# Where one query tile is loaded, and how five others are dealt out, in a two-block kernel with a gathered expert layer

## The chip, the cores and the metric

The kernel runs on one core of one Trainium2 chip. Its engines are TensorE (PE, with PEld for its weight loads), VectorE (DVE), ScalarE (ACT), GpSimd (POOL) and SyncE (SP, which only issues transfers here); 16 DMA engines move the data. The metric is the device time of one execution in microseconds (us). Before the change it is 1383.3 us, the median of three runs (1383.12 to 1384.93).

## What is computed

Two transformer blocks, one after the other, on 256 tokens of width 1024, all in float32. The part that this change touches is the second half of the first block, a product-key expert layer ("PEER"). Cut to what matters, the reference is:

```python
q = h @ wq                                   # h: normed x, 256 x 1024; wq: 1024 x 2048 (8 heads x 2 x 128)
s1, s2 = q[.., 0] @ keys[h, 0].T, q[.., 1] @ keys[h, 1].T      # 128 scores on each side
v1, i1 = top_k(s1, 16); v2, i2 = top_k(s2, 16)
top_s, pos = top_k(v1[:, None] + v2[None, :], 16)              # 16 best pairs of 256
idx = i1 * 128 + i2;  g = softmax(top_s)                        # 8 heads x 16 = 128 experts a token
a = <u[idx], h>;  x = x + sum(gelu(a) * g * v[idx])             # u, v: 16384 x 1024 each
x = x + sigmoid(norm(x) @ ple_gate) * (p @ ple_proj)            # "PLE", right behind it
```

Each token needs 128 rows of `u` and of `v`. They lie side by side in one table, so an expert's row has 2048 floats (8 KB).

## The kernel before, in words

The 256 tokens are two blocks of 128 (b = 0, 1), one token on each of 128 partitions. Each block needs 128 gathers. Gather k fetches, for every token of the block, the table row of one of its experts: 128 rows of 8 KB, 1.05 MB. The 256 gathers are issued one by one by POOL (line L1421) into a ring of ten places in SBUF (`pair_ring`; gather k goes to place (k + 1) mod 10, so k = 7 and 8 go to places 8 and 9, and k = 9 to place 0). Gather k of 10 or more waits until TensorE is done with gather k - 10 (`pair_free`).

Four gathers are a batch (64 batches, m = 0 to 63; block 0 has batches 0 to 31). For each batch VectorE takes four dot products with `u` (L1824), forms the weights with one tanh of ScalarE between (L1229), ScalarE builds four diagonal matrices (L1235), and TensorE multiplies each with `v` and adds to two PSUM banks (L804: two matmuls of 128x512 a gather, eight a batch).

Which rows to fetch comes from the routing: queries (TensorE), scores against the keys (TensorE, L759), and top-k searches (VectorE, L1726 to L1791). The 2048 query columns are four tiles, `peer_q0` to `peer_q3`, each for a pair of heads, 1024x512 floats (2 MB). The routing of a block is thus four parts (b, q). In block 0, parts (0,0), (0,1) and (0,2) are multiplied ahead of the first batch, whole. The other five are dealt out: after each batch TensorE does a quarter of a query product (`dealt`, L748, eight matmuls of 128x128), and after four quarters the scores. VectorE's search pieces are dealt out in the same way (`route_list`). All engines run their instructions in the order written; nothing is rescheduled.

Weight tiles come through a ring of three places (`wring`, 2 MB each), loaded by SP in the order of `tile_list` (L451). A tile is issued once the tile three before it in that list has had its last use. In the list the tiles here are `out0`, `out1` (the projection ahead of the expert layer), `peer_q0` to `peer_q3`, `ple_proj` (1 MB), `ple0`, `ple1`, and then tiles of the second block. So `peer_q2` can be issued only when `out1` has had its last product, and `peer_q3` when `peer_q0` has had the one for block 1.

Of the kernel before, what the change touches and what calls it, by code (L numbers as in the profile page):

```python
# [20 lines left out]
P = 128  # L21
S = 256
NB = S // P
D = 1024
KD = D // P
# [19 lines left out]
ADA_PARTS = (0, 1, 2, 3, 6, 7, 8, 9, 4, 5, 10, 11)  # L45
ADA_COLS = 8
FF_ADA = {1: 10, 2: 11}
PLE_PROJ, PLE_TURN, PLE_GATE, PLE_NORM, PLE_LAST = 36, 35, 40, 51, 54
GELU_C = 0.7978845608028654


# [25 lines left out]
def route_list():  # L77

    after = {}
    starts = {(0, 1): 0, (0, 2): 6, (0, 3): 14, (1, 0): 20, (1, 1): 26, (1, 2): 34, (1, 3): 42}  # L80
    for (b, q), m in starts.items():
        for piece, step in enumerate((0, 1, 2, 3, 4) if m == 0 else (0, 1, 3, 4, 5)):
            after.setdefault(m + step, []).append((b, q, piece))
    return after
# [2 lines left out]
ROUTE_AFTER = route_list()  # L87
BEST_AFTER = {m: p[:2] for m, pieces in ROUTE_AFTER.items() for p in pieces if p[2] == 3}

QUERY_FROM = {1: (1, 0), 5: (1, 1), 9: (0, 3), 14: (1, 2), 19: (1, 3)}  # L90

SEARCH = [(b, q) for b in range(NB) for q in range(PAIRS)]
SC_SLOT = {(0, 0): 0, (0, 1): 1, (0, 2): 2, (1, 0): 3, (0, 3): 0, (1, 1): 1, (1, 2): 2, (1, 3): 0}
# [3 lines left out]
def tile_list():  # L97


    ada = [(f"ada{i}", KD, 512, "w_ada", 0, 512 * ADA_PARTS[i]) for i in range(12)]  # L100
    at, t_in = 0, {}
    for n, w in (("q", 512), ("kv", 256), ("hq", 512), ("hf", 512), ("hb", 512), ("hi", 512), ("hg", 512),
                 ("g0", 512), ("g1", 512), ("g2", 512), ("g3", 512)):
        t_in[n] = ("in_" + n, KD, w, "w_in", 0, at)
        at += w
    t = [t_in[n] for n in ("hf", "hb", "q", "kv", "hq", "hi", "hg")]
    t += [ada[0], ada[1], t_in["g0"], ada[2], t_in["g1"], ada[3], t_in["g2"], ada[4], t_in["g3"], ada[5]]
    t += [("up_att", 4, D, "w_up_att", 0, 0)] + ada[6:ADA_COLS]
    t += [(f"out{i}", KD, 512, "w_out", 0, 512 * i) for i in range(2)]
    t += [(f"peer_q{i}", KD, 512, "peer_wq", 0, 512 * i) for i in range(4)]  # L110
    t += [("ple_proj", 2, D, "ple_proj", 0, 0)]
    t += [(f"ple{i}", KD, 512, "ple_gate", 0, 512 * i) for i in range(2)]
    t += [("in2_" + n, KD, 512, "w_in_2", 0, 512 * i) for i, n in enumerate(("q", "k", "v", "qm", "km"))]
    t += [("in2_if", KD, 64, "w_if", 0, 0), ("in2_vm", KD, 512, "w_in_2", 0, 512 * 5), ada[8]]
    t += [("in2_og", KD, 512, "w_in_2", 0, 512 * 6)] + ada[9:10]
    t += [(f"out2_{i}", KD, 512, "w_out_2", 0, 512 * i) for i in range(2)]
    for i in range(6):
        w = min(512, FF - 512 * i)
        t += [(f"gate{i}", KD, w, "w_gate", 0, 512 * i), (f"up{i}", KD, w, "w_up", 0, 512 * i)]
        if i in FF_ADA:  # L120
            t += [ada[FF_ADA[i]]]
    t += [(f"down{i}", min(4, FC - 4 * i), D, "w_down", 512 * i, 0) for i in range(6)]
    return t
# [6 lines left out]
def product_list():  # L130
# [4 lines left out]
    def half(n, b):  # L135
        return [(n, b, h) for h in range(2)]
# [23 lines left out]
    p += [("out0", 0), ("ada_col",), ("out1", 0)]  # L160
    p += half("n2T", 0) + [("out0", 1), ("peer_q0", 0, 0), ("keys", 0, 0, 0), ("peer_q0", 0, 1), ("keys", 0, 0, 1), ("out1", 1)]
    p += [("peer_q1", 0), ("peer_q2", 0), ("keys", 0, 1), ("keys", 0, 2)] + half("n2T", 1)
    for b, q in QUERY_FROM.values():
        p += [(f"peer_q{q}", b), ("keys", b, q)]
    p += half("experts", 0)
    p += half("n3T", 0) + [("ple_proj", b, h) for b in range(NB) for h in range(2)] + [("ple0", 0), ("ple1", 0)]
    p += half("n4T", 0) + half("experts", 1)
    p += half("n3T", 1) + [("ple0", 1), ("ple1", 1), ("in2_q", 0), ("in2_k", 0)] + half("n4T", 1)
# [46 lines left out]
def two_blocks(nc, a, out):  # L215

    with ExitStack() as ctx:
# [67 lines left out]
            return (k + 1) % RING  # L285

        sc = {pair: at(big, 20480 + 512 * n, 512).rearrange("p (n k) -> p n k", n=4) for pair, n in SC_SLOT.items()}
        subkeys = at(big, 22528, 2 * PH * NKEYS)
        h2T = [at(big, lo, D).rearrange("p (c t) -> p c t", c=KD) for lo in (26048, 27072)]
        pqT = at(big, 28096, 512).rearrange("p (n t) -> p n t", n=4)  # L290
# [72 lines left out]
        down_used, ada_used = sem("down_used"), sem("ada_used")  # L363
        x_landed = [sem(f"x_landed{b}") for b in range(NB)]
        ident_landed, const_landed, lane_landed = sem("ident_landed"), sem("const_landed"), sem("lane_landed")
        keys_landed = sem("keys_landed")
        rows_landed, mask_landed, pT_landed = sem("rows_landed"), sem("mask_landed"), sem("pT_landed")
        gain_landed, row_landed, row_added = sem("gain_landed"), sem("row_landed"), sem("row_added")
        ms_ready, rstd_ready, h_ready = sem("ms_ready"), sem("rstd_ready"), sem("h_ready")
# [57 lines left out]
        def _(sp):  # L427
# [3 lines left out]
            for n, (name, k, w, src, r0, c0) in enumerate(TILES):  # L431
# [12 lines left out]
                    sp.dma_start(up_hg, a["w_up_hg"].rearrange("(c p) n -> p c n", p=P)).then_inc(up_hg_landed, 16)  # L444
                if name == "in2_q":
                    sp.wait_ge(pair_free, (BATCHES - 1) * BATCH - 2)
                if name == "out0":
                    wait_product(sp, "g_A", 0, 1)
                    sp.dma_start(subkeys, a["subkeys"]).then_inc(keys_landed, 16)
                slot = n % W_SLOTS * TILE  # L450
                sp.dma_start(wring[:, slot:slot + k * w].rearrange("p (c n) -> p c n", c=k),  # L451
                             a[src][r0:r0 + k * P, :].rearrange("(c p) n -> p c n", p=P)[:, :, c0:c0 + w])\
                  .then_inc(tile_landed[n % W_SLOTS], 16)
                if n == 0:
                    sp.dma_start(x[:, 1, :], a["x"][P:S, :]).then_inc(x_landed[1], 16)
                if n == 1:
# [13 lines left out]
        def _(pe):  # L470
# [268 lines left out]
                pe.wait_ge(h_ready, 3 + b)  # L739
                turn("n2T", h_t, [b])  # L740

            def query(name, b, parts=range(4)):

                wt = tile(name, KD, 512)
                o = begin(name, b) if parts[0] == 0 else ps[:, BANK[(name, b)], :]
                for n in parts:
                    for c in range(KD):
                        last = nc.tensor.matmul(o[:, n * P:(n + 1) * P], wt[:, c, n * P:(n + 1) * P], h2T[b][:, c, :],  # L748
                                                start=(c == 0), stop=(c == KD - 1))
                if parts[-1] == 3:  # L750
                    last.then_inc(product_done, 1)

            def score(b, q):
# [66 lines left out]

            def dealt(m):
                for m0, (b, q) in QUERY_FROM.items():
                    if 0 <= m - m0 < 4:
                        query(f"peer_q{q}", b, range(m - m0, m - m0 + 1))
                    elif m - m0 == 4:
                        score(b, q)

            for m in range(1, HALF_BATCHES):
# [25 lines left out]

            for m in range(HALF_BATCHES, BATCHES):
                experts(m, banks)
                if m == PLE_TURN:
                    pe.wait_ge(h_ready, 5)
                    turn("n3T", h_t, [0])
                    pe.wait_ge(pT_landed, 16)  # L860
# [212 lines left out]
        def _(act):  # L1073
# [179 lines left out]
            def query_dealt(m):  # L1253

                for m0, (b, q) in QUERY_FROM.items():
                    if m - 1 == m0 + 3:
                        query_out(b, q)
                    if m - 1 == m0 + 4:
                        scores_out(b, q)

            exp_and_tanh()
# [22 lines left out]
            for m in range(HALF_BATCHES, BATCHES):  # L1284
# [3 lines left out]
                if m == HALF_BATCHES + 1:  # L1288
                    log_and_exp()
                    rms(2, 0)  # L1290
                    exp_and_tanh()
                if 0 <= m - 1 - PLE_PROJ < 4:
                    b, h = (m - 1 - PLE_PROJ) // 2, (m - 1 - PLE_PROJ) % 2
                    move(pp[:, b, h * 512:(h + 1) * 512], "ple_proj", b, h)
# [94 lines left out]
        def _(pool):  # L1389
# [22 lines left out]
            for k in range(NB * SLOTS):  # L1412
                if k == SLOTS // PAIRS // 2:
                    pool.wait_ge(indexed, 2)
                elif k % (SLOTS // PAIRS) == 0:
                    pool.wait_ge(indexed, k // (SLOTS // PAIRS) + (2 if k else 1))
                if ring_at(k) == 0 and k < RING:
                    wait_product(pool, "out1", 1)
                if k >= RING:
# [733 lines left out]
```

## Time and profile before

| | |
|---|---|
| median of three runs | 1383.3 us |
| the profiled execution's own time | 1384.18 us |
| its span (first to last instruction) | 1382.4 us |
| PE busy | 1241.1 us (90%) |
| DVE busy | 741.8 us (54%) |
| ACT busy | 231.6 us (17%) |
| POOL busy | 324.2 us (23%) |
| software-issued DMA queue (the gathers) | 270.29 MB |
| hardware-issued DMA queue (all weight tiles) | 127.88 MB |

The profile is of one execution on the chip. The granted clock is TensorE's, as a share of full speed. A wait for several semaphores is put down to the one that came last. The gathers run from 277 us to about 955 us of the span, so this stage is half of the kernel. A busy share averaged over the whole span says little about one stage; the rows below are therefore mostly of that stage.

### The profile page before, as it was taken

What the parts mean: (1) busy time and instruction counts of PE and PEld (TensorE: products, weight loads), DVE (VectorE), ACT (ScalarE), POOL (GpSimd) and SP (SyncE); (2) the same over time, 40 slices, a digit from 0 to 9 for tenths busy, and PEclk for the clock granted to TensorE, in tenths of its full rate; (3) what the DMA queues carried; (4) which work ended last, traced back from release to release, by engine and by line L of the source; (5) the groups of instructions that cost most, each with busy time, mean ns of one, the idle gap of its engine ahead of it and who ended that gap; (6) DMA issues with size and microseconds to landing.
All of it is one profiled execution on the core that took longest, in us unless ns stands there. A gap on an engine that the chain in (4) does not pass through costs nothing.

```text
span 1382.4 us, 12732 instructions
## 1 busy us (share of the span) xinstructions
PE 1241.1 (90%) x4624; PEld 742.5 (54%) x4624; DVE 741.8 (54%) x1777; ACT 231.6 (17%) x596; POOL 324.2 (23%) x273
## 2 busy tenths in 40 slices
PE   6999999978889888778798887787999899999998
PEld 6766887554444444323343333333466558888743
DVE  2766633369676777777786865653244632230001
ACT  2132210111211111112221112111201421000000
POOL 0100000034444445354445445451000000000000
PEclk9999999999999999999899999889999899999999
DMA  8445587299999999999999999996435324564531
GB/s 293 154 153 183 183 304 290 69 385 397 382 420 421 421 416 421 416 421 418 421 412 422 408 413 421 419 420 257 137 129 191 138 112 163 181 244 132 195 144 39
DMA packets 98670, 398.99 MB, mean 289 GB/s; under 512 B 6384, under 2 KB 9840, under 8 KB 65712
## 3 DMA queue, kind: packets, MB, share of 16 engines
q0 software_dynamic: 37376, 270.29, 47.5%
q1 hardware_dynamic: 61232, 127.88, 25.9%
q8 instruction: 38, 0.62, 0.2%
q14 instruction: 24, 0.20, 0.0%
HBM read 397.10 MB, written 1.05 MB: 288 GB/s over the span
## 4 chain that ended last, share of the span: by engine, by line
PE 59%; DMA 23%; DVE 13%; ACT 2%; issue 2%; POOL 1%; SPq 0%; DVEq 0%; ACTq 0%
DMA big<-in_peer_uv,idx_t 21%; PE ps L521 17%; PE ps L509 10%; PE ps L804 10%; DVE big L1824 6%; PE ps L1064 5%; PE ps L619 3%; PE ps L694 2%; PE ps L1024 2%; PE ps L537 1%; PE ps L748 1%; DMA wring<-in_peer_wq 1%; PE ps L600 1%; PE ps L725 1%; POOL big L1421 1%
## 5 line engine op out<-in xcount | busy, mean ns | idle before, releaser
L804 PE MATMUL ps<-big,rows 128*128 128x512 f32 x1024 | 487.1, 632 | 110.6 <-ACT rows L1235 110.6
L804 PEld LDWEIGHTS ps<-big,rows 128*128 128x128 f32 x1024 | 201.7, 202 | 378.3 <-issue 378.1
L1421 POOL DMA_INDIRECT big<-in_peer_uv,idx_t x256 | 311.1, 1215 | 382.6 <-PE ps L804 331.5
L1824 DVE CUSTOM_DVE_ANT_0 big<-big 128x1024 f32<-128x1024 f32 x256 | 307.9, 1224 | 146.2 <-DMA big<-in_peer_uv,idx_t 142.8
L521 PE MATMUL ps<-big,wring 128*128 128x256 f32 x1088 | 237.4, 379 | 0.0
L521 PEld LDWEIGHTS ps<-big,wring 128*128 128x128 f32 x1088 | 205.9, 190 | 31.4 <-issue 3.9
L509 PE MATMUL ps<-wring,big 128*128 128x512 f32 (+1 forms) x336 | 142.4, 581 | 4.4 <-DVE big L1950 4.4
L509 PEld LDWEIGHTS ps<-wring,big 128*128 128x128 f32 x336 | 64.1, 193 | 75.9 <-issue 74.5
L1229 ACT ACTIVATE small<-small 128x4 f32<-128x4 f32 x64 | 13.2, 206 | 507.5 <-DVE small L1829 507.5
L1235 ACT ACTIVATE rows<-const,small 128x128 f32<-128x128 f32 x256 | 81.8, 390 | 19.6 <-DVE small L1833 18.4
L1064 PE MATMUL ps<-wring,big 128*128 128x512 f32 x176 | 75.7, 592 | 0.0
L1432 POOL TENSOR_TENSOR big<-big,rows 128x1024 f32<-128x1024 f32 x2 | 5.1, 2539 | 291.4 <-ACT big L1109 291.4
L748 PEld LDWEIGHTS ps<-big,wring 128*128 128x128 f32 x448 | 55.1, 198 | 17.0 <-issue 9.1
L748 PE MATMUL ps<-big,wring 128*128 128x128 f32 x448 | 55.5, 281 | 7.8 <-DMA wring<-in_peer_wq 7.8
L1109 ACT ACTIVATE big<-ps 128x512 f32<-128x512 f32 (+1 forms) x65 | 35.1, 579 | 124.6 <-PE ps L509 27.0
L1064 PEld LDWEIGHTS ps<-wring,big 128*128 128x128 f32 x176 | 33.4, 190 | 41.7 <-issue 41.6
L2016 DVE SCALAR_TENSOR_TENSOR big<-ps,big 128x512 f32<-128x512 f32 x8 | 5.5, 692 | 92.7 <-PE ps L1064 70.6
L2059 DVE TENSOR_TENSOR big<-big,ps 128x512 f32<-128x512 f32 x11 | 7.6, 688 | 82.1 <-PE ps L521 74.8
L619 PE MATMUL ps<-big,wring 128*128 128x128 f32 x384 | 45.4, 281 | 4.0 <-DMA wring<-in_w_in 3.0
L619 PEld LDWEIGHTS ps<-big,wring 128*128 128x128 f32 x384 | 44.9, 198 | 5.1 <-issue 3.9
L1401 POOL DMA_DIRECT2D rows<-in_norm_ffn x1 | 0.7, 686 | 138.8 <-DVE big L1677 138.8
L1024 PE MATMUL ps<-wring,big 128*128 128x512 f32 x64 | 28.0, 592 | 0.0
(251 smaller groups left out, 923.0 us busy)
## 6 DMA issues: line engine op xcount, KB each, us to landing
wring<-in_w_in SPq DMA_DIRECT2D x17, 2048.0 KB, 8.4
wring<-in_w_ada SPq DMA_DIRECT2D x12, 2048.0 KB, 8.3
wring<-in_w_gate SPq DMA_DIRECT2D x5, 2048.0 KB, 7.8
wring<-in_w_up SPq DMA_DIRECT2D x5, 2048.0 KB, 7.7
wring<-in_w_down SPq DMA_DIRECT2D x5, 2048.0 KB, 7.8
wring<-in_w_out SPq DMA_DIRECT2D x4, 2048.0 KB, 8.8
wring<-in_peer_wq SPq DMA_DIRECT2D x4, 2048.0 KB, 10.1
big<-in_peer_uv,idx_t POOLq DMA_INDIRECT x256, 13.4
```

The costliest lines, as they stand in the source:

```text
L509: last = nc.tensor.matmul(o[:, 0:w], lhs[:, c, b * P:(b + 1) * P], wt[:, c, c0:c0 + w], start=(c == 0), stop=(c == k - 1))
L521: last = nc.tensor.matmul(o[:, c2 * S:(c2 + 1) * S], wt[:, c, n0:n0 + P], src[:, c, :], start=(c == 0), stop=(c == KD - 1))
L619: last = nc.tensor.matmul(o[:, c2 * S + b * P:c2 * S + (b + 1) * P], wt[:, c, n0:n0 + P], src[:, c, b * P:(b + 1) * P], start=(c == 0), st ...
L694: last = nc.tensor.matmul(o[:, c2 * S:(c2 + 1) * S], wt[:, c, n0:n0 + P], lhs[:, c, :], start=(c == 0), stop=(c == 3))
L748: last = nc.tensor.matmul(o[:, n * P:(n + 1) * P], wt[:, c, n * P:(n + 1) * P], h2T[b][:, c, :], start=(c == 0), stop=(c == KD - 1))
L804: last = nc.tensor.matmul(banks[h], diag[:, k % DIAGS, :], v_part[:, ring_at(k), h * 512:(h + 1) * 512], start=False, stop=(k % SLOTS == S ...
L1024: last = nc.tensor.matmul(o, hT2[:, c, b * P:(b + 1) * P], wt[:, c, :], start=(c == 0), stop=(c == KD - 1))
L1064: last = nc.tensor.matmul(o, gT[:, f, b * P:(b + 1) * P], wt[:, c, h * 512:(h + 1) * 512], start=(f == 0), stop=(f == FC - 1))
L1109: nc.scalar.activation(dst, bank(name, n) if src is None else src, ACT.Copy).then_inc(emptied(*name), 1)
L1235: nc.scalar.activation(diag[:, k % DIAGS, :], ident, ACT.Copy, scale=w_now[:, at_w:at_w + 1])\
L1421: pool.indirect_dma_start(pair_ring[:, ring_at(k), :], None, a["peer_uv"], bass.IndirectOffsetOnAxis(idx_t[:, k:k + 1], 0))\
L1824: nc.vector.tensor_tensor_reduce(u_part[:, ring_at(k), :], u_part[:, ring_at(k), :], h_t[:, b, :], 1.0, 0.0, ALU.mult, ALU.add, a_dot[:, i ...
```

## The change

It has four edits, all in the expert stage.

1. The tile `peer_q2` for block 0 gets its own load, issued behind `peer_q0`, once the small product `ada_col` is done. It goes to the place of ring rows 8 and 9 (`q2_home`), which the gathers k = 7 and 8 use first. These two gathers (and k = 9 behind them in POOL's order) wait until the block-0 product with `peer_q2` is done.
2. In the list of ring tiles, `peer_q3` now comes ahead of `peer_q2`. `peer_q3` waits for the last use of `out1` and also for the landing of gather k = 9. `peer_q2` is loaded a second time, for block 1, behind it. One tile more is loaded in all.
3. The five dealt queries are in the order (0,3), (1,0), (1,1), (1,2), (1,3) instead of (1,0), (1,1), (0,3), (1,2), (1,3), each in eighths (four matmuls) over eight batches, from batches 1, 9, 17, 25 and 33, instead of in quarters from batches 1, 5, 9, 14 and 19. The search pieces of (1,1), (1,2) and (1,3) start two batches later.
4. The PLE steps move from batches 35 to 54 to batches 41 to 59, with the same distances but for one: the projection now starts in the batch of the transpose instead of the one behind it.

The core of the diff:

```diff
-PLE_PROJ, PLE_TURN, PLE_GATE, PLE_NORM, PLE_LAST = 36, 35, 40, 51, 54
+PLE_PROJ, PLE_TURN, PLE_GATE, PLE_NORM, PLE_LAST = 41, 41, 45, 56, 59
-    starts = {(0, 1): 0, (0, 2): 6, (0, 3): 14, (1, 0): 20, (1, 1): 26, (1, 2): 34, (1, 3): 42}
+    starts = {(0, 1): 0, (0, 2): 6, (0, 3): 14, (1, 0): 20, (1, 1): 28, (1, 2): 36, (1, 3): 44}
-QUERY_FROM = {1: (1, 0), 5: (1, 1), 9: (0, 3), 14: (1, 2), 19: (1, 3)}
+QUERY_FROM = {1: (0, 3), 9: (1, 0), 17: (1, 1), 25: (1, 2), 33: (1, 3)}
+PIECES = 8
-    t += [(f"peer_q{i}", KD, 512, "peer_wq", 0, 512 * i) for i in range(4)]
+    t += [(f"peer_q{i}", KD, 512, "peer_wq", 0, 512 * i) for i in (0, 1, 3, 2)]
+        q2_home = at(big, 8 * 2 * D, TILE).rearrange("p (c n) -> p c n", c=KD)
...
+                if name == "peer_q3":
+                    sp.wait_ge(pair_landed[ring_at(RING - 1)], 16)
...
+                if name == "peer_q0":
+                    wait_product(sp, "ada_col")
+                    sp.dma_start(q2_home, a["peer_wq"].rearrange("(c p) n -> p c n", p=P)[:, :, 2 * 512:3 * 512])\
+                      .then_inc(q2_landed, 16)
...
-            def query(name, b, parts=range(4)):
-                wt = tile(name, KD, 512)
-                o = begin(name, b) if parts[0] == 0 else ps[:, BANK[(name, b)], :]
-                for n in parts:
-                    for c in range(KD):
+            def query(name, b, pieces=range(PIECES)):
+                if (name, b) == ("peer_q2", 0):
+                    pe.wait_ge(q2_landed, 16)
+                    wt = q2_home
+                else:
+                    wt = tile(name, KD, 512)
+                o = reserved(name, b) if pieces[0] == 0 else ps[:, BANK[(name, b)], :]
+                for piece in pieces:
+                    n, c0 = piece // 2, piece % 2 * 4
+                    for c in range(c0, c0 + 4):
...
+                if ring_at(k) in (8, 9) and k < RING:
+                    wait_product(pool, "peer_q2", 0)
```

On SyncE, the issues from the last `w_out` tile to the two `ple_gate` tiles. Before (`wring` is the weight ring, `in_peer_wq` the query weights):

```order
L451 DMA wring<-in_w_out 128x8x512 [waits ada_used]
L451 DMA wring<-in_peer_wq 128x8x512 [waits product_done] x4
L451 DMA wring<-in_ple_proj 128x2x1024 [waits product_done]
L451 DMA wring<-in_ple_gate 128x8x512 [waits product_done] x2
L451 DMA wring<-in_w_in 128x8x512 [waits pair_free,product_done]
```

After (`pair_landed0` is raised by gather k = 9):

```order
L456 DMA wring<-in_w_out 128x8x512 [waits ada_used]
L456 DMA wring<-in_peer_wq 128x8x512 [waits product_done]
L461 DMA big<-in_peer_wq 128x8x512 [waits product_done]
L456 DMA wring<-in_peer_wq 128x8x512 [waits product_done]
L456 DMA wring<-in_peer_wq 128x8x512 [waits pair_landed0,product_done]
L456 DMA wring<-in_peer_wq 128x8x512 [waits product_done]
L456 DMA wring<-in_ple_proj 128x2x1024 [waits product_done]
```

Five issues of query weights stand where four stood; the fourth of them, `peer_q3`, is tied to a gather's landing.

On TensorE, batch 1 (the last of its gathers), the dealt piece behind it, and the first gather of batch 2. Before:

```order
L804 MATMUL ps<-big,rows 128x512 [waits diag_built,pair_landed8]
L804 MATMUL ps<-big,rows 128x512
L748 MATMUL ps<-big,wring 128x128 [waits bank_emptied1,tile_landed1]
L748 MATMUL ps<-big,wring 128x128 x7
L804 MATMUL ps<-big,rows 128x512 [waits diag_built,pair_landed9]
```

After:

```order
L819 MATMUL ps<-big,rows 128x512 [waits diag_built,pair_landed8]
L819 MATMUL ps<-big,rows 128x512
L762 MATMUL ps<-big,wring 128x128 [waits bank_emptied1,tile_landed0]
L762 MATMUL ps<-big,wring 128x128 x3
L819 MATMUL ps<-big,rows 128x512 [waits diag_built,pair_landed9]
```

The piece behind batch 1 has half the matmuls, and it reads place 0 of the weight ring, where `peer_q3` lands, instead of place 1, where `peer_q0` has lain since before the stage. All of batch 2 stands behind it.

On POOL, the first gathers. Before:

```order
L1421 DMA big<-in_peer_uv,idx_t 128x2048 [waits indexed]
L1421 DMA big<-in_peer_uv,idx_t 128x2048 x8
L1421 DMA big<-in_peer_uv,idx_t 128x2048 [waits product_done]
L1421 DMA big<-in_peer_uv,idx_t 128x2048 [waits pair_free] x6
L1421 DMA big<-in_peer_uv,idx_t 128x2048 [waits pair_free,indexed]
```

After:

```order
L1440 DMA big<-in_peer_uv,idx_t 128x2048 [waits indexed]
L1440 DMA big<-in_peer_uv,idx_t 128x2048 x6
L1440 DMA big<-in_peer_uv,idx_t 128x2048 [waits product_done] x3
L1440 DMA big<-in_peer_uv,idx_t 128x2048 [waits pair_free] x6
L1440 DMA big<-in_peer_uv,idx_t 128x2048 [waits pair_free,indexed]
```

Seven gathers instead of nine are free of a wait for a product; k = 7 and 8 now wait for that of `peer_q2`, k = 9 for that of `out1` as before.

## Rows read from the trace of the kernel before

**Rows 1.** The page: the chain of waits, by engine and by line.

```profile
PE 59%; DMA 23%; DVE 13%; ACT 2%; issue 2%; POOL 1%; SPq 0%; DVEq 0%; ACTq 0%
```

**Rows 2.** Windows: stretch; busy us of PE, PEld, DVE, ACT, POOL; clock; DMA share; GB/s.

```profile
276.00:308.00 32.00, 22.85 (x150) 19.47 (x149) 21.37 (x80) 6.19 (x14) 11.21 (x11) 0.89 0.96 387
308.00:332.00 24.00, 21.32 (x74) 11.30 (x73) 21.66 (x65) 4.42 (x13) 12.35 (x10) 1.00 0.98 371
332.00:348.00 16.00, 12.46 (x51) 7.39 (x50) 14.88 (x41) 3.09 (x11) 5.61 (x6) 0.96 1.01 421
348.00:364.00 16.00, 16.00 (x49) 8.02 (x48) 10.10 (x28) 2.95 (x10) 8.80 (x7) 0.94 0.90 344
690.00:712.00 22.00, 22.00 (x50) 9.42 (x49) 19.50 (x54) 4.16 (x13) 10.70 (x11) 0.97 1.00 405
790.00:800.00 10.00, 9.33 (x22) 4.00 (x21) 9.42 (x23) 1.48 (x5) 4.91 (x4) 0.98 0.95 347
800.00:944.00 144.00, 116.23 (x247) 48.77 (x246) 86.01 (x194) 25.58 (x77) 69.81 (x58) 0.92 1.01 421
```

**Rows 3.** Timeline of PE: start us, us, engine, line, operation, tiles, [idle before, releaser].

```profile
276.42 7.31 PE L748 MATMUL ps<-big,wring 128*128 128x128 f32 x64
291.49 9.28 PE L748 MATMUL ps<-big,wring 128*128 128x128 f32 x64 [7.76 <-DMA wring<-in_peer_wq]
300.61 1.06 PE L759 MATMUL ps<-big 128*128 128x128 f32 x8
304.77 7.10 PE L804 MATMUL ps<-big,rows 128*128 128x512 f32 x16 [1.39 <-ACT rows L1235]
315.31 7.11 PE L804 MATMUL ps<-big,rows 128*128 128x512 f32 x16 [1.67 <-ACT rows L1235]
322.25 1.95 PE L748 MATMUL ps<-big,wring 128*128 128x128 f32 x16
346.52 8.80 PE L804 MATMUL ps<-big,rows 128*128 128x512 f32 x16 [2.02 <-ACT rows L1235]
```

**Rows 4.** Timeline of DVE: last dot product and weights of batch 0; of a later batch.

```profile
295.01 1.23 DVE L1824 CUSTOM_DVE_ANT_0 big<-big 128x1024 f32<-128x1024 f32 x1 [1.25 <-DMA big<-in_peer_uv,idx_t]
304.02 0.16 DVE L1833 SCALAR_TENSOR_TENSOR small<-small 128x4 f32<-128x4 f32 x1 [7.11 <-ACT small L1229]
...
772.71 1.23 DVE L1824 CUSTOM_DVE_ANT_0 big<-big 128x1024 f32<-128x1024 f32 x1 [1.26 <-DMA big<-in_peer_uv,idx_t]
...
774.88 0.16 DVE L1833 SCALAR_TENSOR_TENSOR small<-small 128x4 f32<-128x4 f32 x1 [0.27 <-ACT small L1229]
```

**Rows 5.** Timeline of POOL: gathers k = 0, 10 and 26.

```profile
277.32 1.04 POOL L1421 DMA_INDIRECT big<-in_peer_uv,idx_t  x1 [27.89 <-DVE idx_t L1781]
306.99 0.94 POOL L1421 DMA_INDIRECT big<-in_peer_uv,idx_t  x1 [16.67 <-PE ps L804]
350.43 1.53 POOL L1421 DMA_INDIRECT big<-in_peer_uv,idx_t  x1 [5.94 <-PE ps L804]
```

**Rows 6.** DMA queues in 281 to 282 us: packets, MB, share.

```profile
q1 hardware_dynamic: 188, 0.39, 99.8%
q0 software_dynamic: 7, 0.06, 13.8%
```

**Rows 7.** DMA queues in 370 to 376 us.

```profile
q0 software_dynamic: 262, 1.88, 76.7%
q1 hardware_dynamic: 262, 0.54, 23.4%
```

**Rows 8.** The same view, 382 to 388 us: the end of that tile.

```profile
q1 hardware_dynamic: 115, 0.20, 9.0%
```

**Rows 9.** Half-microsecond windows around gather k = 26 (columns of rows 2).

```profile
351.50:352.00 0.50, 0.50 (x2) 0.19 (x1) 0.30 (x3) 0.20 (x1) 0.47 (x1) 1.00 0.19 82
352.50:353.00 0.50, 0.50 (x2) 0.19 (x1) 0.50 (x1) 0.50 (x3) 0.50 (x1) 1.00 1.32 229
```

**Rows 10.** The chain: start us, us, what (the load of `peer_q2`).

```profile
276.62 14.37 DMA wring<-in_peer_wq
```

**Rows 11.** SP's issue of `peer_q3` at 357.1 us: issue to landing.

```profile
L451 SPq DMA_DIRECT2D wring<-in_peer_wq x1: 367/367/367, 357.1 to 357.1; - x1
DMA to landing us min/median/max: 29.7/29.7/29.7
```

**Rows 12.** Timeline of DVE at 780 us: second half of a PLE addition.

```profile
780.43 0.69 DVE L1853 SCALAR_TENSOR_TENSOR x_t<-big,x_t 128x512 f32<-128x512 f32 x1
```

More of the change, by code:

```diff
@@ L162, in product_list @@
     p += [("peer_q1", 0), ("peer_q2", 0), ("keys", 0, 1), ("keys", 0, 2)] + half("n2T", 1)
-    for b, q in QUERY_FROM.values():
+    for m0, (b, q) in QUERY_FROM.items():
+        if m0 + PIECES - 1 == HALF_BATCHES:
+            p += half("experts", 0)
         p += [(f"peer_q{q}", b), ("keys", b, q)]
-    p += half("experts", 0)
     p += half("n3T", 0) + [("ple_proj", b, h) for b in range(NB) for h in range(2)] + [("ple0", 0), ("ple1", 0)]
@@ L365, in two_blocks @@
         ident_landed, const_landed, lane_landed = sem("ident_landed"), sem("const_landed"), sem("lane_landed")
-        keys_landed = sem("keys_landed")
+        keys_landed, q2_landed = sem("keys_landed"), sem("q2_landed")
         rows_landed, mask_landed, pT_landed = sem("rows_landed"), sem("mask_landed"), sem("pT_landed")
@@ L740, in turn_query @@
                 turn("n2T", h_t, [b])
-            def query(name, b, parts=range(4)):
-                wt = tile(name, KD, 512)
-                o = begin(name, b) if parts[0] == 0 else ps[:, BANK[(name, b)], :]
-                for n in parts:
-                    for c in range(KD):
+            def query(name, b, pieces=range(PIECES)):
[8 more added lines that the diff above has]
+                    for c in range(c0, c0 + 4):
                         last = nc.tensor.matmul(o[:, n * P:(n + 1) * P], wt[:, c, n * P:(n + 1) * P], h2T[b][:, c, :],
                                                 start=(c == 0), stop=(c == KD - 1))
-                if parts[-1] == 3:
+                if pieces[-1] == PIECES - 1:
+                    begin(name, b)
                     last.then_inc(product_done, 1)
@@ L822, in dealt @@
                 for m0, (b, q) in QUERY_FROM.items():
-                    if 0 <= m - m0 < 4:
+                    if 0 <= m - m0 < PIECES:
                         query(f"peer_q{q}", b, range(m - m0, m - m0 + 1))
-                    elif m - m0 == 4:
+                    elif m - m0 == PIECES:
                         score(b, q)
@@ L856, in _ @@
                 experts(m, banks)
+                dealt(m)
                 if m == PLE_TURN:
@@ L1255, in query_dealt @@
                 for m0, (b, q) in QUERY_FROM.items():
-                    if m - 1 == m0 + 3:
+                    if m - 1 == m0 + PIECES - 1:
                         query_out(b, q)
-                    if m - 1 == m0 + 4:
+                    if m - 1 == m0 + PIECES:
                         scores_out(b, q)
@@ L1291, in _ @@
                     exp_and_tanh()
+                query_dealt(m)
                 if 0 <= m - 1 - PLE_PROJ < 4:
```

## The prediction, as it was put on record

> **What bounds the kernel now.** I read the chain of waits first. It gives TensorE 59%, DMA 23% and VectorE 13% [rows 1], which is an average over stages. So the next view is the table of windows over the expert stage [rows 2]. The reader is to see that the DMA share is 1.01 wherever the rate is 421 GB/s (332 to 348 us, 800 to 944 us), while PE and DVE have idle time there. The stage is bound by the bytes that it moves, and its length is bytes divided by 421 GB/s plus the time in which DMA is short of work. An edit there can gain only what lies in such shortages, or lose by making new ones. They are, at 421 GB/s: 308 to 332 us, 24 x (421 - 371) / 421 = 2.9 us; 348 to 364 us, 16 x 77 / 421 = 2.9 us; 690 to 712 us, 22 x 16 / 421 = 0.8 us; 790 to 800 us, 10 x 74 / 421 = 1.8 us [rows 2]. That is 8.4 us, the most that can be had in this stage. The third view is the timeline of the start of the stage [rows 3 to 5], where TensorE stands still 7.76 us for `peer_q2` [rows 3].
>
> **The wait that goes.** With `peer_q2` landed early, its product follows that of `peer_q1` at 283.7 us and takes 7.31 us instead of 9.28. The first scores end at about 292 instead of 301.7 us [rows 3]. Batch 0 then depends on VectorE: its last dot product started at 295.01, and the weights came only at 304.02, because ScalarE stood behind those scores [rows 4]. Without them in the way the weights come 0.9 us after the last dot product, as in a later batch (772.71 + 1.23 to 774.88) [rows 4], and L804 follows 0.75 us behind (304.02 to 304.77) [rows 3, 4]. That dot product ends at about 294 us (k = 3 lands at 292.7, below), so I put the first L804 at 295.8 instead of 304.77. Batch 1 followed batch 0 by 10.54 us [rows 3], so it starts at about 306.4 and ends at 313.5. TensorE is 9 us ahead. But in this stage that is no gain in itself: ahead of 308 us DMA was busy all the time with ten gathers and the tile.
>
> **Bytes.** A tile is 2.1 MB, 5.0 us at 421 GB/s; a gather is 1.05 MB, 2.49 us. The stage before moves `peer_q2`, `peer_q3`, `ple_proj`, `ple0`, `ple1` beside the gathers; the stage after moves `peer_q3`, `peer_q2` (block 1), and the same last three. The extra tile is loaded ahead of the stage, from about 246 us, and costs nothing. So the bytes in the stage are the same.
>
> **The start (+).** Gather k = 0 was issued at 277.32 [rows 5], and in 281 to 282 us the gathers had moved only 7 packets [rows 6], so their first bytes came 4.4 us after the issue. Gather k = 26 was issued at 350.43 [rows 5] into a queue that ran dry, and bytes came at about 352.5 [rows 9], 2.1 us after. Before the change `peer_q2` filled this hole. Now nothing does: gathers alone start at 279.4 to 281.7; I take 280.5. POOL holds k = 7 to 9 until the product with `peer_q2` ends at 291; seven gathers keep DMA busy until 280.5 + 17.4 = 297.9, so that wait is covered, by 2 us even if their bytes come 4.4 us after the issue.
>
> **The new wait.** `peer_q3` is issued when k = 9 has landed: 280.5 + 10 x 2.49 + 2.2 = 307.6 us. The 2.2 us from last byte to landing are those of `peer_q3` before: at 43.7 packets a us [rows 7] its last 115 packets end at 384.6 [rows 8], and it landed at 357.1 + 29.7 = 386.8 [rows 11]. (So k = 3 lands at 280.5 + 10.0 + 2.2 = 292.7.) TensorE wants it behind batch 1, at 313.5, and batch 2 with its freeing of ring places is queued behind that piece. How soon does it land? In 370 to 376 us a tile and gathers shared the engines packet for packet, 262 and 262, that is 0.54 MB for the tile and 1.88 MB for the gathers [rows 7]. A tile has 1024 pieces of 2 KB, so it lasts as long as about 1024 pieces of 8 KB, which is eight gathers. Eight gathers are just what can be in flight: batches 0 and 1 free eight places, k = 10 to 17, and no more come until batch 2. Tile and gathers thus end together, when all 18 gathers and the tile are through: 280.5 + 20 x 2.49 = 330.3 us. With 2.2 us to the landing the tile is there at 332.5, 25 us after its issue. TensorE stands still for 19 us.
>
> The Trainium skill says otherwise of the sharing. In "DMA: Bandwidth & Descriptors", section "Queues, rings and completion order", a DMA engine drains a whole packet of one queue, typically 9 to 17 descriptors, before it turns to the next. With packets of many 2 KB pieces on the tile's side and less on the gathers' side, the tile would get the greater share and land early. The row speaks for one piece against one.
>
> **DMA runs dry (+).** From 330.3 us no gather is left. After the landing TensorE needs the dealt piece (half of 1.95 us at full clock, 1.95 at half) and the first gather of batch 2. From the start of a batch to the next gather's issue it took 2.22 us at full clock (304.77 to 306.99) and 3.91 us at 346.52 to 350.43, where the batch took 8.80 instead of 7.10 us [rows 3, 5]. After the 7.76 us of idling before, 64 matmuls took 9.28 instead of 7.31 us [rows 3], so after 19 us I take the slow values: 332.5 + 1.95 + 3.91 = 338.4, and 2.1 us to the bytes: gather k = 18 gets its first byte at 340.5 us. Before the change the same 20 units (18 gathers and one tile, 21.0 MB) were through at 331.2 us: 32 x 387 + 24 x 371 makes 21.3 MB by 332 us [rows 2]. So the stage is 9.3 us later there. Ends: 329.2 + 2.2 + 0.98 + 2.22 + 2.1 = 336.7 (+5.5), and 331.5 + 2.2 + 1.95 + 3.91 + 4.4 = 344.0 (+12.8).
>
> **What comes back (-).** The shortage at 348 to 364 us followed a start with VectorE as slow as DMA (batch 1 started 10.54 us behind batch 0, with search pieces in each) and a slow clock. During the new stall VectorE gets ahead, and TensorE has batches 2 and 3 waiting, at 8.1 us each with eighths against 9.96 us of DMA. I take all 2.9 us as gone (between 0 and 2.9). The shortage at 790 to 800 us stands where a PLE addition [rows 12] fell between two search pieces of (1,3); now those pieces are in batches 44 to 49 and the additions in 50 and 54, so I take its 1.8 us as gone (0 to 1.8). The one at 690 us is the change of blocks and stays (0 to 0.8). The eighths themselves are worth nothing: TensorE's pieces lie beside gathers. `ple0` and `ple1` are now issued together at the end of batch 40; at 29.7 us each they are there some 3 and 6 batches later, ahead of batches 45 and 49. The moved PLE steps lie beside gathers too, and batch 41, with scores, transpose and projection at about 11 us, is carried by the ring. The work behind batch 63 is unchanged.
>
> **Sum.** 9.3 - 2.9 - 1.8 = +4.6 us, with ends of 0 (5.5 - 2.9 - 1.8 - 0.8) and +12.8. The profiled execution took 1384.2 us, 0.9 above the median of 1383.3. So 1388.8 against it, and 1388 us against the median.
>
> **Rivals.** (a) Faster: `peer_q3` lands early. For: `peer_q2` before landed 14.37 us after its issue [rows 10], and on an engine with few gathers queued a tile could take more. Against: much of that load moved before the gathers did (188 packets against 7) [rows 6], and `peer_q3` before shared packet for packet [rows 7, 11]. Then it lands at 307.6 + 14.4 = 322.0, TensorE frees places from 326, and DMA never runs dry. The stage then loses nothing but the start (280.5 + 49.8 = 330.3 against 331.2, so -0.9) and gets back 2.9, 1.8 and perhaps 0.8: -5.6 to -6.4, 1377.5 us against the median. The page's rule of whole packets would give just this. It decides if the landing is ahead of about 324 us. (b) No change: the stall is there, but its price is at the low ends (TensorE's clock full, short latency) and all shortages go: 0 to +2, 1384.5 us against the median. (c) Slower by much: the dry spell costs its high end and nothing comes back, since VectorE's search pieces of (0,2) in batches 6 to 11 meet a ring that has just been refilled and make a shortage like that of 348 us: between +9.3 and +12.8, near 1394 us against the median.
>
> **Chances.** The forecast 0.55, (a) 0.18, (b) 0.17, (c) 0.10. About 0.2% (2.8 us) is what a measurement of this kernel can tell from no change. The forecast's own range is 1384.5 to 1392. Slower: most of the forecast and all of (c), 0.6. Faster: (a), 0.18. Same: 0.22. The range that leaves no more than 2 in 10 out takes in most of (a) and (c) and runs from 1377.5 to 1394 us.
>
> **What would show it.** In the profile after: L762 of `peer_q2` right behind that of `peer_q1` (if not, the first step is wrong); the first L819 near 296 us; SP's issue of `peer_q3` near 307 and its landing near 332; TensorE idle some 19 us ahead of the piece behind batch 1, put down to DMA of `peer_wq`; windows in 330 to 340 us with a DMA rate near zero; 421 GB/s from 341 us and through 790 to 800 us. The forecast is wrong if that landing is ahead of 324 us, or if DMA stays full while TensorE waits.

## The result, and the profile after

The changed kernel took 1390.5 us (median of 7 runs, 1384.4 to 1393.1); the kernel before, beside it, 1383.3 us (7 runs, 1380.0 to 1389.1). The ratio is 1.0045, with a 95% interval of 1.0027 to 1.0063. Timed once more among the experiments it was 1.0023 (1.0010 to 1.0037). It is slower, by 3 to 7 us: the medians are 7.2 and 3.2 us apart in the two timings, and the ratios say 6.2 and 3.2. The profiled execution took 1386.67 us (before 1384.18). It is the second fastest of its seven, so the two profiles are only 2.5 us apart.

The timeline of PE after answers to [rows 3]: the product with `peer_q1`, that with `peer_q2` in three pieces, the first scores, batches 0 and 1, the dealt piece, batch 2 (start us, us, engine, line, operation, [idle before, releaser]).

```profile
276.43 7.31 PE L762 MATMUL ps<-big,wring 128*128 128x128 f32 x64
283.58 1.61 PE L762 MATMUL ps<-big 128*128 128x128 f32 x13
285.81 0.38 PE L762 MATMUL ps<-big 128*128 128x128 f32 x2 [0.61 <-issue]
287.22 5.63 PE L762 MATMUL ps<-big 128*128 128x128 f32 x49 [1.03 <-issue]
292.69 1.06 PE L774 MATMUL ps<-big 128*128 128x128 f32 x8
...
296.85 7.11 PE L819 MATMUL ps<-big,rows 128*128 128x512 f32 x16 [1.39 <-ACT rows L1251]
...
307.39 7.10 PE L819 MATMUL ps<-big,rows 128*128 128x512 f32 x16 [1.67 <-ACT rows L1251]
332.94 2.07 PE L762 MATMUL ps<-big,wring 128*128 128x128 f32 x8 [18.44 <-DMA wring<-in_peer_wq]
334.81 7.88 PE L819 MATMUL ps<-big,rows 128*128 128x512 f32 x16
```

The wait of 7.76 us for `peer_q2` is gone and batch 0 is 7.9 us earlier. Then TensorE stands still for 18.44 us, behind batch 1, ahead of a dealt piece of 2 us. What that does to the gathers is in the windows after, in the columns of [rows 2]:

```profile
276.00:308.00 32.00, 27.29 (x176) 21.48 (x175) 27.68 (x98) 9.00 (x22) 15.46 (x14) 1.00 0.90 365
308.00:332.00 24.00, 6.50 (x16) 2.56 (x14) 21.35 (x65) 3.21 (x12) 5.21 (x4) 0.74 0.96 388
332.00:348.00 16.00, 15.06 (x43) 8.19 (x44) 6.13 (x11) 0.00 (x0) 5.40 (x6) 0.86 0.54 195
348.00:364.00 16.00, 14.01 (x45) 7.18 (x44) 8.93 (x24) 2.97 (x10) 8.17 (x8) 1.00 1.01 424
690.00:712.00 22.00, 18.91 (x51) 9.27 (x52) 16.72 (x52) 4.28 (x15) 9.77 (x9) 0.92 1.01 420
780.00:800.00 20.00, 18.74 (x37) 8.22 (x38) 13.99 (x41) 3.44 (x11) 7.78 (x7) 0.83 1.00 397
800.00:944.00 144.00, 123.31 (x262) 51.62 (x261) 96.33 (x231) 27.42 (x84) 69.93 (x57) 0.92 1.01 415
```

332 to 348 us moved 195 GB/s where it moved 421 before. Finer windows show the hole. The rate falls from 329 us on, is nearly nothing from 331 us, and is back between 340 and 341 us:

```profile
328.00:331.00 3.00, 0.00 (x0) 0.00 (x0) 2.80 (x10) 1.40 (x5) 0.00 (x0) 0.50 0.84 330
331.00:332.00 1.00, 0.00 (x0) 0.00 (x0) 0.93 (x3) 0.00 (x0) 0.00 (x0) 0.50 0.11 45
332.00:340.00 8.00, 7.06 (x19) 4.12 (x20) 3.66 (x7) 0.00 (x0) 1.42 (x2) 0.72 0.11 18
340.00:341.00 1.00, 1.00 (x4) 0.51 (x3) 0.00 (x0) 0.00 (x0) 0.46 (x1) 1.00 0.76 287
```

SP's issue of `peer_q3`, its landing and who waited for it (against [rows 11]), and the first gather behind the hole (against [rows 5]):

```profile
L456 SPq DMA_DIRECT2D wring<-in_peer_wq x1: 368/368/368, 307.7 to 307.7; - x1
...
  PE ps L762: 18.4, 1
...
DMA to landing us min/median/max: 25.2/25.2/25.2
...
337.80 0.94 POOL L1440 DMA_INDIRECT big<-in_peer_uv,idx_t  x1 [21.30 <-PE ps L819]
```

From here on, shortage is the time for which DMA was short of work, with each stretch counted at 421 GB/s. It was 8.4 us of 276 to 364 us before (381 GB/s over 88 us) and 14.6 us after (351 GB/s). Over 364 to 944 us both moved 418 GB/s. The matmuls behind the last batch began at 966.72 us before and at 971.75 after.

### The profile page after: what moved, and what is told of

The parts are those of the page before. It is cut to its first block, busy times and chain, and to the rows that moved or that the text cites. A ratio compares the mean times of both kernels' runs of the same rounds, so it can differ in the third digit from the quotient of the medians.

```text
span 1384.9 us, 12735 instructions
## 1 busy us (share of the span) xinstructions
PE 1240.5 (90%) x4624; PEld 742.9 (54%) x4624; DVE 741.5 (54%) x1777; ACT 231.2 (17%) x596; POOL 327.7 (24%) x273
## 3 DMA queue, kind: packets, MB, share of 16 engines
HBM read 399.20 MB, written 1.05 MB: 289 GB/s over the span
## 4 chain that ended last, share of the span: by engine, by line
PE 58%; DMA 27%; DVE 10%; issue 2%; POOL 2%; ACT 2%; SPq 0%; DVEq 0%; ACTq 0%
DMA big<-in_peer_uv,idx_t 24%; PE ps L530 17%; PE ps L518 10%; PE ps L819 9%; PE ps L1080 5%; DVE big L1843 5%; PE ps L628 3%; PE ps L703 2%; PE ps L1040 2%; DMA wring<-in_peer_wq 2%; POOL big L1440 2%; PE ps L546 1%; PE ps L762 1%; PE ps L609 1%; PE ps L734 1%
## 5 line engine op out<-in xcount | busy, mean ns | idle before, releaser
L1440 POOL DMA_INDIRECT big<-in_peer_uv,idx_t x256 | 314.6, 1229 | 384.7 <-PE ps L819 325.3
L530 PEld LDWEIGHTS ps<-big,wring 128*128 128x128 f32 x1088 | 205.9, 190 | 31.4 <-issue 4.0
L762 PEld LDWEIGHTS ps<-big,wring 128*128 128x128 f32 x384 | 49.7, 194 | 36.5 <-DMA wring<-in_peer_wq 19.3
L762 PE MATMUL ps<-big,wring 128*128 128x128 f32 x384 | 50.5, 278 | 18.4 <-DMA wring<-in_peer_wq 18.4
L628 PE MATMUL ps<-big,wring 128*128 128x128 f32 x384 | 45.4, 282 | 4.0 <-DMA wring<-in_w_in 3.0
L628 PEld LDWEIGHTS ps<-big,wring 128*128 128x128 f32 x384 | 45.0, 198 | 5.1 <-issue 3.9
```

What stands on the lines that cost most here:

```text
L530: last = nc.tensor.matmul(o[:, c2 * S:(c2 + 1) * S], wt[:, c, n0:n0 + P], src[:, c, :], start=(c == 0), stop=(c == KD - 1))
L628: last = nc.tensor.matmul(o[:, c2 * S + b * P:c2 * S + (b + 1) * P], wt[:, c, n0:n0 + P], src[:, c, b * P:(b + 1) * P], start=(c == 0), st ...
L1440: pool.indirect_dma_start(pair_ring[:, ring_at(k), :], None, a["peer_uv"], bass.IndirectOffsetOnAxis(idx_t[:, k:k + 1], 0))\
```

## The experiments

Each kernel was timed in five rounds beside the kernel before. All differ from the changed kernel (A) or the kernel before (B) by the edit shown. The ratios are not quotients of the two medians given and can differ from them by up to 0.0014, about 2 us, so differences of 1 or 2 us between the runs below say nothing. The theory is that the loss is the time in which DMA has no gather to work on, made by the wait for `peer_q3` at batch 1, and nothing else of the change.

**No wait for a gather (A).**

```diff
-                if name == "peer_q3":
-                    sp.wait_ge(pair_landed[ring_at(RING - 1)], 16)
```

> The changed kernel, but SyncE no longer waits for the landing of gather k = 9 before it issues peer_q3; it goes out when out1 has had its last product, near 276.6 us, as peer_q2 did before the change. Theory 1 (the loss is the stall behind batch 1, in which DMA runs dry, and nothing else): the tile lands near 291 us, TensorE does not wait for it at batch 1, DMA is full from 279 to past 690 us, gather k = 18 gets its first byte near 329 us instead of 341, and the time is 2.3 + 2.9 us below the kernel before: 1378 us, about 12 us less than the changed kernel. Theory 2 (the loss comes from the smaller, more frequent pieces or from the later PLE steps): the stall goes, but the time stays within 2 us of the changed kernel. Theory 3 (loading a tile ahead of the first gathers delays their landing and batch 0 by as much as is won): batch 0 starts near 304 us again and the time is near 1383 us.

Measured: 1379.5 us, ratio 0.9974 (0.9960 to 0.9988). The tile was issued at 277.6, landed in 14.6 us, and nobody waited for it. Its windows:

```profile
276.00:308.00 32.00, 27.68 (x176) 21.46 (x174) 27.19 (x91) 6.98 (x16) 15.41 (x14) 1.00 0.92 374
308.00:332.00 24.00, 18.10 (x54) 9.08 (x54) 21.95 (x74) 5.24 (x18) 11.28 (x9) 1.00 1.01 422
332.00:348.00 16.00, 13.09 (x33) 6.10 (x32) 12.92 (x28) 1.48 (x5) 6.21 (x6) 0.89 1.01 419
```

Two lines of the change, taken away, turn it from slower to faster than before. The eighths and the later PLE steps are still in it, so theory 2 falls. Part of theory 3 holds, without a price: the last dot product of batch 0 waited for its gather until 296.26 us (in A it ran at 292.87), and batch 0 began at 299.18 instead of 296.85, but DMA was at 422 GB/s behind 308 us.

**The pieces one batch later (A).** `QUERY_FROM = {2: (0, 3), 9: (1, 0), ...}` instead of `{1: (0, 3), ...}`.

> The changed kernel with one number changed: the pieces of the query (0,3) go behind batches 2 to 9 instead of 1 to 8; the load of peer_q3 stays tied to gather k = 9. Theory 1 (what costs is not that TensorE waits, but that no gather is in flight while it does): peer_q3 is issued near 307.7 and lands near 332.9 us as in the changed kernel, TensorE waits for it some 8 to 9 us behind batch 2, but batch 2 has freed four more places, so that gathers last until about 340 us and DMA never runs dry. The time falls by the whole dry spell of about 10 us less what it hid, to 1379 to 1381 us. Theory 2 (TensorE's standing still is what costs): half of the wait stays, so about half of the loss, near 1386 us. Theory 3 (the pieces or the PLE steps are to blame): no change from the changed kernel.

Measured: 1381.3 us, 0.9989 (0.9974 to 1.0004). TensorE waited 9.46 us, half as long as in A, but the tile came at 335.6, and a hole of 5 us was left, at 340 to 352 us:

```profile
336.00:340.00 4.00, 4.00 (x11) 2.47 (x11) 2.67 (x6) 0.00 (x0) 0.00 (x0) 0.50 1.01 420
340.00:344.00 4.00, 4.00 (x9) 1.81 (x8) 2.79 (x10) 1.48 (x5) 2.34 (x2) 0.85 0.11 47
344.00:348.00 4.00, 4.00 (x17) 2.29 (x16) 0.54 (x2) 0.00 (x0) 3.23 (x3) 1.00 1.02 324
348.00:352.00 4.00, 4.00 (x11) 1.84 (x10) 1.62 (x3) 0.00 (x0) 1.96 (x2) 1.00 0.98 375
```

My expectation had left out that some 8 us pass from the tile's landing to the next bytes. The time is that of theory 1 and well below the 1386 us of theory 2. But the hole and the wait of TensorE have both shrunk by about half, so this run alone doesn't tell which of the two costs.

**Two batches later (A).** `{3: (0, 3), 9: (1, 0), ...}`.

> The changed kernel with the pieces of the query (0,3) behind batches 3 to 10 instead of 1 to 8, peer_q3 still tied to gather k = 9. With one batch later DMA was still short of work for a few us in 332 to 348 us, since TensorE took some 6 us from the tile's landing to the next freed place. Theory (only time in which DMA has no gather costs): with two batches ahead of the first piece the gathers in flight last until about 350 us, the tile lands near 336, and DMA is full from 281 to past 690 us. TensorE waits for the tile at most 2 us. Time 1379 to 1381 us, a ratio near 0.998, like the run that waits for k = 3. If a shortage stays in 332 to 364 us, the count of gathers in flight is not what decides.

Measured: 1381.4 us, 0.9997 (0.9983 to 1.0010). The trace is as expected: no wait for the tile, 422 GB/s in 332 to 348 and 420 in 348 to 364 us, and the last batch was through at 963.6 us, against 971.75 in A. The median is near those of the other kernels without a hole, but the kernel before ran at 1381.2 beside it (1382.5 and 1383.3 in the other two sets), and the ratio missed the expected 0.998. It is below both of A's (1.0023 and 1.0045), so the loss is gone. That something is won against the kernel before, it doesn't show.

**Waiting for k = 3 instead of k = 9 (A).** `sp.wait_ge(pair_landed[ring_at(3)], 16)`.

> The changed kernel, but peer_q3 waits for the landing of gather k = 3 instead of k = 9 and is issued near 292.7 us. Theory 1 (packet for packet, so it lasts as long as eight gathers): it lands near 318 to 321 us, TensorE waits 5 to 7 us behind batch 1, but the gathers k = 12 to 17 last until 330 us, TensorE frees places from about 325, and DMA never runs dry for more than 1 us. The time falls by 7 to 10 us against the changed kernel, to 1379 to 1381 us, although TensorE still waits. Theory 2 (any wait of TensorE behind batch 1 costs its length): the wait of 6 us keeps a third of the loss, near 1386 us.

Measured: 1380.8 us, 0.9981 (0.9968 to 0.9993). TensorE waits and DMA doesn't:

```profile
319.62 2.07 PE L762 MATMUL ps<-big,wring 128*128 128x128 f32 x8 [5.00 <-DMA wring<-in_peer_wq]
```

```profile
308.00:332.00 24.00, 19.00 (x53) 9.71 (x52) 20.62 (x64) 3.33 (x12) 9.66 (x8) 0.93 1.02 419
332.00:348.00 16.00, 13.10 (x30) 6.04 (x29) 12.10 (x28) 1.48 (x5) 5.53 (x6) 0.79 1.01 419
```

A wait of 5.00 us ahead of the same piece cost nothing that can be measured: the loss of A is gone altogether. This run, and not the one with the pieces a batch later, separates a standing TensorE from a standing DMA.

**Waiting for k = 13 (A).** `sp.wait_ge(pair_landed[ring_at(13)], 32)`.

> The changed kernel, but peer_q3 waits for the landing of gather k = 13 instead of k = 9, so it is issued about 10 us later, near 317.6. Theory 1 (the tile shares packet for packet, and once the gathers in flight are used up it has the engines alone; what counts is when all 18 gathers and the tile are through, and that is the same): the tile lands at about 333 to 335 us, only 0 to 2 us later than with k = 9 (332.9), and the time is 0 to 2 us above the changed kernel. Theory 2 (a tile issued in this stage takes some 25 us from its issue, whatever is beside it): it lands near 343 us, the dry spell grows by 10 us, and so does the time, to about 1399 us.

Measured: 1386.3 us, 1.0029 (1.0015 to 1.0043), the same as A timed beside it. The tile was issued 9.2 us later, at 316.9, and landed at about the same time, 332.3 against 332.9:

```profile
DMA to landing us min/median/max: 15.4/15.4/15.4
```

The reason is in its DMA queues from 320 to 330 us (packets, MB, share). The gathers ran out in this stretch, and the tile had the engines alone (in 328 to 330 us, 371 of its packets went by against 1 of the gathers):

```profile
q1 hardware_dynamic: 950, 1.94, 52.0%
q0 software_dynamic: 289, 2.06, 49.8%
```

In A, from 314 to 328 us, both had work, and as many packets of the one as of the other went by, as in [rows 7]:

```profile
q0 software_dynamic: 616, 4.51, 78.0%
q1 hardware_dynamic: 620, 1.27, 23.9%
```

In A too the gathers ran out first: of the tile's 1040 packets, the last 246 went by from 329 us on, beside 31 of the gathers. So here the landing is set by when all that is in flight is through, and not by the issue. Theory 2 of this run falls.

**The changed kernel again (A, no edit).**

> The changed kernel as it is, timed again beside the others of this call so that they have a common measure. The first timing gave a ratio of 1.0045 (1.0027 to 1.0063) against the kernel before. Expected by every theory: within 1.003 and 1.006, so 1386 to 1391 us, with TensorE idle 18.4 us ahead of the piece behind batch 1, and DMA nearly empty from about 331 to 340 us.

Measured: 1386.5 us, 1.0023 (1.0010 to 1.0037); TensorE waited 18.22 us. The expected ratio was a little higher. In this execution the product with `peer_q2` took 7.31 us without a gap (283.88 to 291.19).

**The late steps alone (B).** The `PLE_...` numbers and the three `starts` of the change.

> The kernel before with only the later steps of the change: PLE steps in batches 41 to 59 and the searches of (1,1), (1,2) and (1,3) two batches later; queries in quarters, tiles and loads as before. Theory 1 as recorded in the prediction: the shortage of 1.8 us at 790 us goes and none comes elsewhere, so 1381.5 us. Rival: the collisions of search pieces and PLE work on VectorE only move (the trace of the changed kernel has shortages near 790 and 885 us), so the time is that of the kernel before, 1383 us. Second rival: the later steps press on the end of the stage, 1385 us or more.

Measured: 1381.1 us, 0.9993 (0.9982 to 1.0004): no difference that can be told. In the trace the shortage at 790 us is gone and another is at 744 to 760 us:

```profile
744.00:748.00 4.00, 4.00 (x13) 1.83 (x12) 1.97 (x7) 1.48 (x5) 2.61 (x2) 1.00 0.88 293
756.00:760.00 4.00, 4.00 (x10) 1.71 (x10) 2.04 (x8) 2.08 (x6) 2.34 (x2) 1.00 0.97 358
780.00:800.00 20.00, 17.77 (x42) 7.56 (x41) 14.81 (x40) 2.96 (x10) 10.78 (x9) 1.00 1.01 421
```

That fits the rival, which said that shortages only move. But it is one execution, and the slowest of the twelve (1384.80 us against a median of 1381.07), so it may show more shortage than the others had.

**The loads alone (B).** The own load of `peer_q2`, the order (0, 1, 3, 2), and the waits of SP, TensorE and POOL, as in the change; queries in quarters in the old order. `peer_q3` is first used at batch 9.

> The kernel before with only the loads of the change: peer_q2 for block 0 in the place of ring rows 8 and 9, peer_q3 ahead of peer_q2 in the list and tied to the landing of gather k = 9; queries in quarters in the old order, (1,0) first, whose tile lies ready; PLE and searches as before. peer_q3 is first used at batch 9, so nobody waits for it. Theory 1: batch 0 starts near 296.9 us, the shortages of 308 to 332 and 348 to 364 us go, DMA starts only at 280.5 us, net -0.9 - 2.9 = -3.8 us, 1379.5 us. Rival (VectorE's search pieces set the pace of the first batches, at 10.5 us against 9.96): part of these shortages comes back, 1382 us.

Measured: 1380.5 us, 0.9995 (0.9980 to 1.0010). The early part is as expected (400 GB/s over 276 to 364 us against 381 before), and batch 0 began at 296.32. The ratio fell short of the forecast gain. In this execution 800 to 860 us moved only 403 GB/s, which may be a part of it. The time leaves a gain open; the trace says that the loads by themselves don't make a hole.

**The loads alone, the tile early (B).** As the last, without the wait for k = 9.

> The kernel before with the loads of the change (peer_q2 for block 0 in the place of ring rows 8 and 9, peer_q3 ahead of peer_q2 in the list), but peer_q3 goes out when out1 is done, without a wait for a gather; queries in quarters, (1,0) first, PLE and searches as before. Theory 1 (what counts is DMA time without work): the tile fills the hole ahead of the first gathers and no shortage comes in the first 90 us, as in the run without the landing wait (-3.6 us). Then the time is that run's, 1378 to 1380 us, a ratio near 0.9975; eighths and later PLE steps are worth nothing by themselves. Rival (the smaller pieces or later PLE steps are worth something): this one is 1 to 3 us slower than that run, 1380 to 1382 us.

Measured: 1380.8 us, 0.9972 (0.9960 to 0.9984). As fast as the first experiment (0.9974) without eighths and late PLE steps: these are worth nothing that can be measured (each interval is about 2 us to either side).

**The same, with the search of (1,3) from batch 40 (B).** `(1, 3): 40` instead of `42`.

> The kernel before with the loads of the change, peer_q3 without a wait for a gather (as in the run of that kind before), and the searches of (1,3) from batch 40 instead of 42, so that the long search pieces of 4.6 and 5.1 us are in batches 43 and 44 and not beside the PLE addition of batch 45. In that earlier run the window 780 to 800 us moved 382 GB/s, a shortage of 1.9 us. Theory (VectorE's collision of search and PLE makes it): the window is at 415 GB/s or more, no new shortage appears, and the time is 1 to 2 us below that run's, a ratio near 0.996. Rival (shortages in the late stage come where TensorE's clock falls at a bad moment, and only move): a shortage of 1 to 3 us appears elsewhere in 700 to 900 us and the ratio stays near 0.997.

Measured: 1378.9 us, 0.9970 (0.9955 to 0.9986). The window 780 to 800 us is full (422 GB/s, against 382 in the run above), so search and PLE work did collide there. But 730 to 750 and 860 to 880 us are at 401 (417 and 413 in the run above), and the ratio is that of the run above, as the rival said. Why shortages come there is not shown. The version that this study leaves is 2 to 4 us faster than the kernel before (by the medians and by the ratio); nothing tells it from the two others near 0.997.

**All runs side by side.** The ratio is that of all timed executions; the other columns are of the one profiled. Shortage is 88 x (421 - rate) / 421 for 276 to 364 us. The end of the last batch is the start of the matmuls behind it.

| kernel | GB/s, 276 to 364 us | shortage, us | GB/s, 364 to 944 us | end of the last batch, us | ratio |
|---|---|---|---|---|---|
| before | 381 | 8.4 | 418 | 966.7 | 1 |
| changed | 351 | 14.6 | 418 | 971.8 | 1.0045 |
| changed, again | 349 | 15.1 | 418 | 972.2 | 1.0023 |
| k = 13 | 353 | 14.2 | 418 | 970.9 | 1.0029 |
| one batch later | 376 | 9.4 | 418 | 966.2 | 0.9989 |
| two batches later | 400 | 4.4 | 416 | 963.6 | 0.9997 |
| k = 3 | 401 | 4.2 | 417 | 963.2 | 0.9981 |
| no wait | 404 | 3.6 | 416 | 962.8 | 0.9974 |
| loads alone | 400 | 4.4 | 416 | 962.8 | 0.9995 |
| loads, tile early | 405 | 3.3 | 416 | 964.9 | 0.9972 |
| same, search earlier | 408 | 2.7 | 416 | 963.9 | 0.9970 |
| late steps alone | 378 | 9.0 | 417 | 970.1 | 0.9993 |

But for the late steps alone, the end of the last batch follows the early shortage. What lies behind it scatters by up to 4 us between the profiles (412.0 to 415.8 us). The early shortage separates the kernels with a hole from the others; among those below 5 us it doesn't order the ratios.

## Why the prediction was right, and which term was not

**The bound.** It held for the loss: what was lost is DMA time without work. In the run for k = 3 TensorE waited 5 us and nothing was lost, and in A it was ahead by 8 us at batch 0 and nothing was won. For gains it is less clear: two runs with 4.4 us of early shortage, 4 us less than before, have ratios of 0.9995 and 0.9997. One reading was incomplete. The prediction called DMA busy all the time ahead of 308 us and left that stretch out of its list of shortages, but at 387 GB/s [rows 2] 276 to 308 us has one of 2.6 us. Its sum of 8.4 us is therefore not the 8.4 us measured here over 276 to 364 us; that the two agree is chance.

**The wait that goes.** Forecast for batch 0: 295.8; measured 296.85. The product with `peer_q2` took 9.3 us in all and not 7.31, because of gaps that the profile puts down to issue; in the second profile of the same kernel it took 7.31, and batch 0 began at 296.07. POOL issued gather k = 7 at 293.13, and DMA moved 426 GB/s from 294 to 298 us, so the gathers in flight covered that wait as forecast.

**The start.** All 18 gathers and the tile were to be through at 330.3; all but 20 of their packets had gone by at 331. The hole ahead of the gathers is there, 365 against 387 GB/s in 276 to 308 us, which is 1.7 us.

**The new wait.** Issue 307.6 forecast and 307.69 measured, landing 332.5 and 332.9, TensorE idle 19 and 18.44 us. Equal numbers of packets, on which the landing stood, were seen in A (616 and 620). The step from there was looser than it reads. By bytes (1.27 MB beside 4.51) a tile lasts as long as seven gathers and not eight, and when its first packets went by, at about 311 us, only some 5.6 gathers were left. So the two did not end together: the gathers ended near 329.5, and the rest of the tile went by alone. The landing came out right because it hangs only on the sum of what is in flight, as the run for k = 13 shows. The rule of the Trainium skill ("DMA: Bandwidth & Descriptors", "Queues, rings and completion order") is that an engine drains a whole packet of about 9 to 17 descriptors from one queue before it turns to the next. The traces here do not refute it, since equal counts over 6 and 14 us don't show in what portions the two alternated. They only show that the tile got no greater share than one of its pieces for one of a gather, and rival (a) needed a greater one.

**DMA runs dry.** The next gather was forecast for 338.4 and issued at 337.80; bytes were forecast for 340.5. The first came between 339.0 and 339.5 us. DMA moved 418 GB/s in 341 to 342 us, and 384 over 341 to 348 us. The piece took 2.07 us, where the next one took 1.05 (at 342.52); the granted clock was 0.50 from 328 to 335 us and 1.00 from 337 us. From the start of batch 2 to the gather's issue 2.99 us passed and not 3.91, and from there to the full rate about 3 us and not 2.1. These two errors cancelled, which was luck.

**What comes back.** The 2.9 us of 348 to 364 us came back (424 GB/s). The 1.8 us of 790 to 800 us did not; that term of the sum failed. 780 to 800 us moved 397 GB/s (383 before), and 800 to 944 us 415 instead of 421, which is 2.1 us; against that, 690 to 712 us won its 0.8 us. Over 364 to 944 us nothing changed (418 and 418). I had found a collision and taken its removal for a gain of the stage. What makes the new shortages stays open. That the moved work makes them is only argued: the loads alone and the loads with the tile early have the same late steps as the kernel before, and they differ from each other as much (411 and 382 GB/s in 780 to 800 us, 414 and 420 in 800 to 944 us).

**The sum.** With that term at zero it is 9.3 - 2.9 = +6.4 us. The shortages of 276 to 364 us grew by 6.2 us, the last batch ended 5.0 us later (the work behind it, which the change does not touch, took 413.2 us instead of 415.7 in these two profiles, by chance), and the ratios of the two timings say +6.2 and +3.2 us. The forecast of +4.6 lies between them, so the time can't tell whether the term was rightly counted; the windows do. That the hole makes the loss is shown by the runs that fill it in three ways (an earlier tile, a later use, the old order), all at or below the time before, and by the run for k = 13, which keeps hole and loss with another issue of the tile. A further cause of less than about 2 us would not have been seen.

## What to carry to other kernels

Where DMA bounds a stage and a ring feeds it, ask of each new wait not how long the waiting engine stands, but how many transfers are in flight while it stands, and when the last of them is through. If the engine that waits for a load is also the one that frees the places for new transfers, ask which ends first. In A the gathers in flight ran out near 329.5 us, before the tile landed at 332.9, and a dry spell of about 9 us followed. In the run for k = 3 the tile was there at 319.6 us, with gathers still in flight, and none did. Tie a load to something only if it would otherwise disturb: here the tile issued at once began in the hole ahead of the first gathers (374 against 365 GB/s in 276 to 308 us) and nobody waited for it.

## What the runs showed of the hardware that I had not expected

- A 2 MB tile landed in 8.5 us when next to nothing moved beside it (the own load of `peer_q2` in A), and in 14.6, 15.4, 25.2, 27.9 or 28.9 us beside gathers (runs without a wait, for k = 13, A, for k = 3, loads alone), the longer the more gathers went by beside it. The one that was issued 9.2 us later landed no later.
- Between the release of the standing TensorE at 332.94 us and full DMA there lay 8 us: a piece at a granted clock of 0.50 (2.07 us), a first gather's matmuls, POOL's issue at 337.80, 1.2 to 1.7 us to the first bytes and about 3 to the full rate.
- The product with `peer_q2`, which read its weights from the places of the gathers, had gaps of 0.61 and 1.03 us in A that the profile puts down to issue. It had none in the run for k = 3 (64 matmuls in 7.31 us) nor in the second profile of A, so it is no property of the kernel. I did not find out why.
